# Four sums of blocks of h by accumulating transfers in a two-layer encoder trunk

## The reference

```
for l in range(DEPTH):                                   # DEPTH = 2
    h = rms_norm(x, norm_g[l])
    proj = jnp.einsum('bsd,de->bse', h, w_in[l])
    (a_u, a_v, a_z, b_q, b_k, b_v, b_z, i_q, i_k, i_w, g_a, g_b) = split_columns(proj)
    y_a = spatial_gating_branch(gelu(a_u), gelu(a_v), a_z, ...)
    att = sparse_attention_branch(q, k, v, qi, ki, i_w, topk)     # top 128 keys of each query
    y_b = att * silu(b_z)
    o_a = jnp.einsum('bse,ed->bsd', y_a, w_oa[l])
    o_b = jnp.einsum('bse,ed->bsd', y_b, w_ob[l])
    merged = sigmoid(g_a + gate_b[l, 0]) * o_a + sigmoid(g_b + gate_b[l, 1]) * o_b
    x = x + jnp.einsum('bsd,de->bse', merged, w_out[l])
```

## Time and profile before

| | |
|---|---|
| median of three runs | 788.47 us (788.38 to 788.62) |
| the profiled execution | 789.69 us, its span 787.9 us |
| TensorE busy | 777.9 us, 99% of the span |
| VectorE busy | 641.4 us, 81% |
| ScalarE busy | 381.6 us, 48% |
| GpSimd busy | 130.3 us, 17% |
| granted TensorE clock, mean | 0.998 |

### The profile page before, as it was taken

One profiled execution on the slowest core, in us unless ns is written; L12 is line 12 of the kernel. 1 busy time (PEld: TensorE's weight loads), 2 busy tenths in 40 slices (PEclk: granted clock), 3 DMA queues, 4 the chain that ended last, 5 costly groups with the idle time before them and its releaser, 6 DMA issues.

```text
span 787.9 us, 11493 instructions
## 1 busy us (share of the span) xinstructions
PE 777.9 (99%) x4124; PEld 669.1 (85%) x4124; DVE 641.4 (81%) x1078; ACT 381.6 (48%) x706; POOL 130.3 (17%) x117
## 2 busy tenths in 40 slices
PE   7999999999999999999999999999999999999998
PEld 7988888888788889988899888888887888899886
DVE  5769999979888767669986799999788887656895
ACT  6566645341344437734664775533324434567242
POOL 1247510000000003012211674000000001120130
PEclk9999999999999999999999999999999999999999
DMA  9635232323231246795873522323232233388584
GB/s 332 221 96 145 82 107 65 97 81 107 80 107 54 66 95 106 191 267 121 186 240 95 174 82 81 107 81 108 68 93 81 82 107 53 81 157 266 139 145 123
DMA packets 44841, 97.89 MB, mean 124 GB/s; under 512 B 3056, under 2 KB 3248, under 8 KB 44784
## 3 DMA queue, kind: packets, MB, share of 16 engines
q1 hardware_dynamic: 32320, 67.12, 27.1%
q0 software_dynamic: 12176, 29.45, 18.2%
q10 hardware_dynamic: 288, 0.59, 0.2%
HBM read 90.85 MB, written 6.29 MB: 123 GB/s over the span
## 4 chain that ended last, share of the span: by engine, by line
PE 86%; DVE 10%; DMA 2%; ACT 1%; issue 1%; DVEq 0%; ACTq 0%; SPq 0%
PE bank L807 17%; PE bank L809 17%; PE bank L808 17%; PE bank L928 5%; PE bank L874 3%; PE bank L876 3%; PE bank L875 3%; PE bank L844 3%; PE bank L845 3%; PE bank L846 3%; PE bank L781 2%; PE bank L799 2%; DVE w_lo L1355 2%; PE bank L737 1%; PE bank L790 1%; DMA x_sb<-in_x 1%
## 5 line engine op out<-in xcount | busy, mean ns | idle before, releaser
L1355 DVE TENSOR_TENSOR w_lo<-w_raw,w_hi 128x1024 fp32r<-128x1024 f32 x144 | 186.7, 1311 | 10.4 <-ACT w_hi L1013 5.6
L1013 ACT ACTIVATE w_hi<-w_raw 128x1024 fp32r<-128x1024 f32 x144 | 148.0, 1054 | 22.2 <-DMA w_raw<-in_w_out 14.6
L807 PE MATMUL bank<-h_lo,w_hi 128*128 128x512 f32 x320 | 128.0, 400 | 0.0
L809 PE MATMUL bank<-h_hi,w_hi 128*128 128x512 f32 x320 | 124.8, 390 | 0.0
L808 PE MATMUL bank<-h_hi,w_lo 128*128 128x512 f32 x320 | 124.6, 389 | 0.0
L807 PE MATMUL bank<-w_lo,h_hi 128*128 128x512 f32 x256 | 100.5, 393 | 0.0
L809 PE MATMUL bank<-w_hi,h_hi 128*128 128x512 f32 x256 | 99.9, 390 | 0.0
L808 PE MATMUL bank<-w_hi,h_lo 128*128 128x512 f32 x256 | 99.9, 390 | 0.0
L686 POOL DMA_DIRECT2D w_raw<-in_w_in x16 | 19.4, 1220 | 408.4 <-DVE w_lo L1355 407.9
L809 PEld LDWEIGHTS bank<-h_hi,w_hi 128*128 128x128 f32 x320 | 60.1, 188 | 12.9
L808 PEld LDWEIGHTS bank<-h_hi,w_lo 128*128 128x128 f32 x320 | 60.2, 188 | 12.3
(11 more groups left out here) (201 smaller groups left out, 1720.6 us busy)
## 6 DMA issues: line engine op xcount, KB each, us to landing
w_raw<-in_w_in SPq DMA_DIRECT2D x92, 512.0 KB, 3.7
w_raw<-in_w_in POOLq DMA_DIRECT2D x16, 512.0 KB, 5.9
w_raw<-in_w_out POOLq DMA_DIRECT2D x16, 512.0 KB, 6.3
w_raw<-in_w_out SPq DMA_DIRECT2D x12, 512.0 KB, 4.2
out<-x_sb POOLq DMA_DIRECT2D x4, 1024.0 KB, 5.9
w_raw<-in_w_oa SPq DMA_DIRECT2D x8, 512.0 KB, 3.2
w_raw<-in_w_ob SPq DMA_DIRECT2D x8, 512.0 KB, 3.9
x_sb<-out POOLq DMA_DIRECT2D x2, 2048.0 KB, 11.5
```

The source lines that it names most:

```text
L807: nc.tensor.matmul(dst, s_h, m_l, start=(n == 0), stop=False)
L809: last = nc.tensor.matmul(dst, s_h, m_h, start=False, stop=(n == len(pairs) - 1))
L1013: nc.scalar.activation(hi, w_raw[:, raw_slot(layer, u)], ACT.Copy).then_inc(s_whi.sem, 1)
L1355: nc.vector.tensor_tensor(lo, w_raw[:, raw_slot(layer, u)], hi.bitcast(F32), ALU.subtract) \
```

## The change

The ten additions a layer on VectorE go. In their place:

- ScalarE copies six blocks a layer, some of them negated, into the places of the sums or into a spare place `h_beside` (memory that the rounded s3 takes later): after jobs VB[2], VB[3], VA[0], VA[1], VA[3] and GA[1].
- GpSimd issues ten accumulating transfers a layer from SBUF to SBUF, 512 KB each, that add the other blocks onto them. They stand after the rope products and before the weight additions for gb. Transfers onto one sum are put one behind the other by waits.
- Signs change: s5, s6 and s4 are now built negated, and rounding and remainder take the sign back (`H_SIGN`).
- ScalarE's roundings wait for the transfers in place of VectorE's sums.
- Two rounds of the top-k of block 3 move from jobs 30 and 31 to jobs 34 and 36.

```
-H_STEPS = {JOB_GA[0]: [0], JOB_GA[1]: [1], JOB_GA[2]: [2, 3], JOB_GA[3]: [4], JOB_GA[4]: [5], JOB_GA[5]: [6],
-           JOB_GA[6]: [7, 8], JOB_GA[7]: [9]}
+H_PARTS = ["-a22 hi to s5", "-a22 lo beside", "a12 hi to s6", "-a11 hi to s3", "-a11 lo beside", "-a11 hi to s4"]
+H_PARTS_AFTER = {JOB_VB[2]: 0, JOB_VB[3]: 1, JOB_VA[0]: 2, JOB_VA[1]: 3, JOB_VA[3]: 4, JOB_GA[1]: 5}
+H_TERMS = {"s5": 3, "s3": 2, "s6": 2, "s4": 3}
+H_SIGN = {"s5": -1.0, "s3": 1.0, "s6": -1.0, "s4": -1.0}
...
-              23: [(2, 1), (3, 2)], 26: [(3, 1)], 28: [(3, 2)], 29: [(3, 1)], **{s: [(3, 1)] for s in range(30, 40)}}
+              23: [(2, 1), (3, 2)], 26: [(3, 1)], 28: [(3, 2)], 29: [(3, 1)], **{s: [(3, 2 if s in (34, 36) else 1)] for s in range(32, 40)}}
...
+                def add_term(name, n, src):
+                    if n > 0:
+                        pool.wait_ge(s_hterm[name].sem, s_hterm[name].at(layer, 16 * n))
+                    pool.dma_start(h_sum_raw(name), src, accum_op=ALU.add).then_inc(s_hterm[name].sem, 16)
+                def part_copied(part):
+                    pool.wait_ge(s_hpart.sem, s_hpart.at(layer, H_PARTS.index(part) + 1))
+                a21_hi, a21_lo = bottom(h_hi).bitcast(F32), bottom(h_lo).bitcast(F32)
+                part_copied("-a22 lo beside")
+                add_term("s5", 0, h_beside[:])
+                part_copied("a12 hi to s6")
+                add_term("s6", 0, top(h_lo, slice(HALF_K, KD)).bitcast(F32))
+                add_term("s5", 1, a21_hi)
+                part_copied("-a11 lo beside")
+                add_term("s3", 0, h_beside[:])
+                add_term("s5", 2, a21_lo)
+                pool.wait_ge(s_hterm["s5"].sem, s_hterm["s5"].at(layer, 48))
+                add_term("s3", 1, h_sum_raw("s5"))
+                pool.wait_ge(s_hterm["s3"].sem, s_hterm["s3"].at(layer, 32))
+                add_term("s6", 1, h_sum_raw("s3"))
+                part_copied("-a11 hi to s4")
+                add_term("s4", 0, h_beside[:])
+                add_term("s4", 1, a21_hi)
+                add_term("s4", 2, a21_lo)
...
             def h_sum_rounded(layer, name):
-                act.wait_ge(s_hsum.sem, s_hsum.at(layer, H_SUMS.index(name) + 1))
+                act.wait_ge(s_hterm[name].sem, s_hterm[name].at(layer, 16 * H_TERMS[name]))
                 if name == "s5":
                     act.wait_ge(s_job.sem, s_job.at(layer, JOB_GA[-1] + 1))
+                    act.wait_ge(s_hterm["s4"].sem, s_hterm["s4"].at(layer, 48))
+                    act.wait_ge(s_hterm["s3"].sem, s_hterm["s3"].at(layer, 32))
+                if name == "s3":
+                    act.wait_ge(s_hterm["s6"].sem, s_hterm["s6"].at(layer, 32))
+                    act.wait_ge(s_hterm["s4"].sem, s_hterm["s4"].at(layer, 16))
...
+            def h_part_copied(layer, i):
+                f, upper = (lambda block: block.bitcast(F32)), slice(HALF_K, KD)
+                if H_PARTS[i] == "-a11 lo beside":
+                    act.wait_ge(s_hterm["s5"].sem, s_hterm["s5"].at(layer, 16))
+                if H_PARTS[i] == "-a11 hi to s4":
+                    act.wait_ge(s_ya.sem, s_ya.at(layer, A_GROUPS))
+                dst, src, sign = [(h_sum_raw("s5"), f(bottom(h_hi, upper)), -1.0), (h_beside[:], f(bottom(h_lo, upper)), -1.0),
+                                  (h_sum_raw("s6"), f(top(h_hi, upper)), 1.0), (h_sum_raw("s3"), f(top(h_hi)), -1.0),
+                                  (h_beside[:], f(top(h_lo)), -1.0), (h_sum_raw("s4"), f(top(h_hi)), -1.0)][i]
+                nc.scalar.activation(dst, src, ACT.Copy, scale=sign).then_inc(s_hpart.sem, 1)
...
-            def h_sum_step(layer, step):
...
-                    (s4, f(top(h_hi)), f(bottom(h_hi)), ALU.subtract), (s4, s4, f(top(h_lo)), ALU.add),
-                    (s4, s4, f(bottom(h_lo)), ALU.subtract),
-                    (s5, f(bottom(h_hi, upper)), f(bottom(h_hi)), ALU.subtract), (s5, s5, f(bottom(h_lo, upper)), ALU.add),
-                    (s5, s5, f(bottom(h_lo)), ALU.subtract),
-                    (s3, s5, f(top(h_hi)), ALU.add), (s3, s3, f(top(h_lo)), ALU.add),
-                    (s6, s3, f(top(h_hi, upper)), ALU.subtract), (s6, s6, f(top(h_lo, upper)), ALU.subtract)]
-                dst, a, b, op = steps[step]
-                vec.link(dve, nc.vector.tensor_tensor(dst, a, b, op))
```

More of the change, by code:

```diff
@@ L99 @@
 GATE_PRODUCTS = ["a11", "a12", "s5", "s3", "s6", "s4", "a22"]
-H_SUMS = ["s4", "s5", "s3", "s6"]
 H_ROUNDED = ["s5", "s3", "s6", "s4"]
@@ L341, in trunk @@
             hs6 = sb("hs6", [P, 2, HALF_K, SEQ // 2], F32R, keep=early)
-        sb("hs3_hi_place", [P, HALF_K, SEQ // 2])
+        h_beside = sb("h_beside", [P, HALF_K, SEQ // 2])
         h3_raw = sb("h3_raw", [P, HALF_K, SEQ // 2])
@@ L406, in trunk @@
         s_gadd = sig("gate_b_bank_added", 6)
-        s_hsum = sig("h_sum_made", 4)
+        s_hpart = sig("h_part_copied", len(H_PARTS))
+        s_hterm = {name: sig(f"h_term_added_{name}", 16 * n, False) for name, n in H_TERMS.items()}
         s_hshi = sig("h_sum_hi_written", 4)
@@ L1241, in beside @@
                     nc.scalar.activation(yb_hi[:, h], z_b[:, h], ACT.Copy).then_inc(s_ybhi.sem, 1)
+                if n in H_PARTS_AFTER:
+                    h_part_copied(layer, H_PARTS_AFTER[n])
                 if n in H_HI_AFTER:
@@ L1347, in _ @@
                  s_ya, s_yalo, s_ma, s_sum, s_mlo, s_max, s_prob, s_yb, s_yblo, s_res, s_blo, s_s5, s_s5lo, s_s6, s_s4, s_slo3,
-                 s_gadd, s_hsum, s_hslo)
+                 s_gadd, s_hslo)
             vec.end_layer(dve)
@@ L1493, in sum_remainder @@
                                                ALU.mult, ALU.subtract).then_inc(s_slo3.sem, 1)
-            def h_sum_step(layer, step):
[L1497 to L1500, removed]
-                    (s4, f(top(h_hi)), f(bottom(h_hi)), ALU.subtract), (s4, s4, f(top(h_lo)), ALU.add),
-                    (s4, s4, f(bottom(h_lo)), ALU.subtract),
-                    (s5, f(bottom(h_hi, upper)), f(bottom(h_hi)), ALU.subtract), (s5, s5, f(bottom(h_lo, upper)), ALU.add),
-                    (s5, s5, f(bottom(h_lo)), ALU.subtract),
-                    (s3, s5, f(top(h_hi)), ALU.add), (s3, s3, f(top(h_lo)), ALU.add),
-                    (s6, s3, f(top(h_hi, upper)), ALU.subtract), (s6, s6, f(top(h_lo, upper)), ALU.subtract)]
-                dst, a, b, op = steps[step]
-                vec.link(dve, nc.vector.tensor_tensor(dst, a, b, op))
-                if step in (2, 5, 7, 9):
-                    dve.sem_inc(s_hsum.sem, 1)
             def h_sum_remainder(layer, name):
@@ L1754, in _ @@
                         topk(n)
-                    for step in H_STEPS.get(n, []):
-                        h_sum_step(layer, step)
                     if n in H_LO_AFTER:
```

6 lines of the change are left out of this document (3 added, 3 removed).

## The result

| | median us | lowest to highest | executions |
|---|---|---|---|
| before | 788.44 | 787.76 to 790.87 | 20 |
| after | 789.37 | 788.25 to 791.49 | 20 |

The ratio is 1.0014, 95% interval 1.0008 to 1.0021: the changed kernel is 0.93 us slower. That is inside the predicted range and under the 0.2% that one such measurement tells from no change, but the interval leaves 1 out.

A forecast was written before the change was run, and what follows sets the result against it. TensorE, busy 777.9 of 787.9 us, was taken as the bound. Every edit was put at 0, so the 788.47 us median gave a forecast of 788.4 us, with a range of 786.6 to 790.2 us.

The forecast's parts named there:

- What bounds the kernel: Whole kernel: TensorE bounds it; VectorE costs the changed part only two 0.88 us stalls before each layer's first attention, 1.76 us.
- Additions removed, worth 0: Jobs GA[0] to GA[7]: twenty additions, 24.5 us of VectorE, lie beside matmuls where TensorE waits for nothing; worth 0.
- So the stall keeps its 0.88 us: worth 0: First attention: the top-k round moved from job 30 stood behind the scaling that releases TensorE, so nothing changes; worth 0.
- The six copies, worth 0: ScalarE, each layer: copies of 1.06 us fit its idle waits; taken as 0, range 0 to 2.9 us.
- The ten transfers, worth 0 inside the span: DMA engines, each layer: accumulating transfers at 6.2 us each land before ScalarE needs the sums; limit 15.4 us; worth 0.
- The issues on GpSimd, worth 0: GpSimd: issues of 1.2 us fit its idle time before 272.13 us and do not hold VectorE; worth 0.
- 787.9 are the span and 1.8 lie around it: Profiled execution of the kernel before, 789.69 us: split into span and the time around it.
- 0 + 0 + 0 + 0: Whole kernel: the sum of the edits' effects, giving a forecast of 788.4 us.
- (1): Before the first attention: VectorE's relief removes the stall, 1.76 us in all, giving 786.7 us; chance 0.08.
- (2): At OA[1]: slow transfers, from 15.4 us each, make ScalarE wait; at 20 us each 804 us; chance 0.03.
- (3): Before the first attention: GpSimd's transfer issues hold VectorE, 4.6 us a layer, giving 797.6 us; chance 0.03.
- (4): VectorE's chain before the first attention: copies or late transfers delay it by up to 2.9 us, 791.4 us; chance 0.06.

The follow-up runs named there:

- g1: Changed kernel with one signal for its transfers and five top-k rounds of block 3 moved behind the first attention (jobs 34 to 38): 788.23 us, ratio 0.9999.
- g3: g1 plus sixteen already satisfied waits (8 instructions) at VectorE's start: 786.93 us, ratio 0.9986.
- e4: Changed kernel without its ten transfers a layer and the waits for them: 789.09 us, ratio 1.0009.
- g0: Kernel before, additions kept on VectorE, with five top-k rounds of block 3 moved from jobs 28 to 31 to jobs 33 to 37: 796.15 us, ratio 1.0094.
- f2: Changed kernel plus sixteen already satisfied waits (8 instructions) at VectorE's start: 789.51 us, ratio 1.0009.
- e2: Kernel before plus six copies a layer on ScalarE into unused memory, without transfers: 788.82 us, ratio 1.0002.
- e3: Kernel before plus ten chained transfers a layer into unused memory, nine accumulating, without copies: 788.30 us, ratio 0.9995.
- f6: Changed kernel with one signal instead of four for its transfers, each waiting for the one before: 788.90 us, ratio 1.0002.
- f9: Changed kernel plus thirty-two already satisfied waits (16 instructions) at ScalarE's start: 789.37 us, ratio 1.0014.
- h1: Changed kernel with its four signals, but each transfer waiting for the end of the one before it: 788.91 us, ratio 1.0005.
- e1: Changed kernel with the two moved top-k rounds back in jobs 30 and 31: 789.35 us, ratio 1.0010.
- g4: g1 plus forty-eight already satisfied waits (24 instructions) at VectorE's start: 787.63 us, ratio 0.9992.

## Why the prediction came out as it did

1. **What bounds the kernel**: right. The five entries of TensorE's waits, the two stalls of 0.88 us as all that VectorE costs in this part, and their worth of 1.76 us: with both gone TensorE gains 1.75 us at the two places in the traces of g1 and g3, and by the clock g3 is 1.3 us faster (its interval allows 0.2 to 2.0).
2. **Additions removed, worth 0**: right for the change as it is. e4, without transfers, has no gain. What the text did not see is how little room was left there (45.9 of 55 us busy before; g0 overran it): the removal is what makes room for the rounds, not a saving.
3. **"So the stall keeps its 0.88 us: worth 0"**: right in layer 0 and off by 0.35 us in layer 1. The step reasoned about which instructions stand ahead, and that was right; what failed is that an instruction's start also depends on its place in the stream. VectorE's stream lost its 20 additions (1058 instructions on the page, before 1078) and their signals and waits, and a 0.35 us pause of its sequencer fell onto the chain, in all five kernels with that stream. f2 took it off again.
4. **The six copies, worth 0**: right (e2: 1.0002). 1.06 us each, and the 3.84 us ahead of z_b are 3.83 still.
5. **The ten transfers, worth 0 inside the span**: right (e3: 0.9995). Landing 4.5 to 10.1 us against the 6.2 taken; the last one ahead of the chain, into s6, is issued at 158.38 us and lands 5.0 us later, at 163.4, for some 164 in the forecast.
6. **The issues on GpSimd, worth 0**: right; 0.85 to 1.87 us each by source (the one row at hand said 1.2), and no stretched instruction on VectorE.
7. **"787.9 are the span and 1.8 lie around it" and the sum "0 + 0 + 0 + 0"**: this is the step that failed most plainly. The 1.8 us were carried over as a constant, without a reason; they are 2.15 in the changed kernel. What makes them so isn't known. f6, with one signal for all transfers, has 1.80 again and a ratio of 1.0002 (0.9993 to 1.0011).

The sum with the measured terms: 788.44 + 0.35 (outside) + 0.35 (stall of layer 1) = 789.14, of 789.37. The other 0.23 us are less than the standard error of the comparison of two such medians; the 0.31 us at 717.6 us would cover them, if the other executions have them too, which no row shows. So the forecast of no change failed by two terms that it put at nothing: the stall, 0.35 us inside the span, and 0.35 us outside it. None of the four rivals came true. The stall did not go (1), no transfer held ScalarE (2), no issue held VectorE (3), and the copies and transfers did not delay the chain (4), though its size, up to 2.9 us, would have covered what was seen.

## What to carry to other kernels

Taking work off an engine that isn't the bound pays nothing by itself; ask at once what can be moved into the room, and read from the stretch's busy time, before and after, whether it fits. Where a change is worth less than a microsecond, its sign is set by things that hang on an instruction's place in the stream: count on some tenths of a us for each such accident, and try the version with a few idle instructions at an engine's start before calling it slower. Compare two executions from one matmul to the next, look at the part of the time outside the span by itself, and see whether the last store lands as fast as the others.

## What the runs showed of the hardware

- Loading instructions is work of the DMA engines, and what lies beside it can be late: the last 256 KB store took 3.2 us with a load of instructions beside it and 2.0 without. The load's place follows VectorE's stream: 8 more VectorE instructions moved its start from after 784 us to between 772 and 774; 16 more on ScalarE (f9) left it where the changed kernel has it, between 778 and 780 us. That the load is what makes the store late rests on two executions of one kernel, and on both going away together in g3 and g4; how a load of 0.3 us costs 1.2 us isn't shown.
- VectorE's sequencer can pause 0.35 us between two of its own instructions (0.43 us in place of 0.08), at a place that a shift of 8 instructions changes. A load of instructions begins 1.7 to 2.0 us behind the end of the pause in after, e4, f6, f9 and h1, and 0.7 us behind it in e1 and g0; that the pause is a matter of loading instructions is a guess.
- An accumulating transfer of 512 KB from SBUF to SBUF is issued in 0.85 to 0.91 us when its source is a plain contiguous tile and in 1.3 to 1.9 us when it is a block of h, and lands in 4.5 to 10.1 us.
- The time outside the span isn't fixed: 1.8 us in fourteen kernels here, 2.0 to 2.2 in five, and in the changed kernel one signal in place of four, with the transfers in a strict chain, took it back.
